# Where the tensors of a decoder kernel lie in SBUF: weights at multiples of 1 KB, activations 512 bytes past one

## The reference

```python
def first_block(x, ...):
    h = rmsnorm(x, g_pre)
    (gq, gk, gv, ga, gz, dq, dk, dv, iq, ik, iw, dz, xq, xz, gates) = split_cols(h @ w_in)   # 11352 columns
    y_gla = gla_mixer(...)      # gated linear attention, chunks of 64
    y_dsa = dsa_mixer(...)      # 128 best keys of each query, then attention
    y_mem = cross_mixer(...)    # attention to 256 memory rows
    merged = (s_gla * (y_gla @ w_gla_out) + s_dsa * (y_dsa @ w_dsa_out)
              + s_mem * (y_mem @ w_x_out))
    return x + rmsnorm(merged @ w_o, g_post)

def second_block(x, ...):       # two layers
    for l in range(2):
        main, mq = mlstm_mixer(...) if l == 0 else swa_mixer(...)
        mix = concat(main, memory_attention(mq, mk, mv)) @ w_out[l]
        x = x + rmsnorm(mix, g_mix_post[l])
        h = rmsnorm(x, g_ffn_pre[l])
        gate, up = split(h @ w_ffn_in[l])                # 1024 -> 2 x 2816
        x = x + rmsnorm((silu(gate) * up) @ w_ffn_out[l], g_ffn_post[l])   # 2816 -> 1024
        if l == 0: k_sh, v_sh = shared_kv(x, ...)
```

## The kernel before, in words

| tensor | start | start modulo 1024 |
|---|---|---|
| raw, whi, wlo | 16512, 32896, 49280 | 128, 128, 128 |
| K (identity, masks) | 65664 | 128 |
| V, gpost, small | 71424, 71872, 75968 | 768, 192, 192 |
| H, XR, R | 78016, 110784, 127168 | 192, 192, 192 |

## Time and profile before

### The profile page before, as it was taken

How to read it: one execution, slowest core, us unless ns; L and a number is a source line. 1 busy time by engine, 2 the same in 40 slices (tenths; PEclk the granted TensorE clock), 3 DMA queues, 4 the chain that set the end, 5 groups by cost and what they waited for, 6 DMA issues and landing times.

```text
span 2001.5 us, 32809 instructions
## 1 busy us (share of the span) xinstructions
PE 1968.7 (98%) x13488; PEld 1781.3 (89%) x13488; DVE 1145.0 (57%) x1595; ACT 932.6 (47%) x1647; POOL 145.5 (7%) x149
## 2 busy tenths in 40 slices
PE   8999999999999999999999999999999999999998
PEld 6798888877889778888999899999988799999998
DVE  3375347465343233353353999972377659999523
ACT  4443142355433342355454755652258856565422
POOL 0000000000000000000000233300000003333000
PEclk9999999999999999999999999999999999999999
DMA  6521122211334123332212233332231113223331
GB/s 179 146 85 64 43 84 84 85 64 59 111 112 162 63 106 105 106 116 89 81 48 80 77 125 106 106 126 95 97 116 43 64 64 116 106 106 106 127 106 64
DMA packets 29824, 191.24 MB, mean 96 GB/s; under 512 B 3689, under 2 KB 4841, under 8 KB 8562
## 3 DMA queue, kind: packets, MB, share of 16 engines
q1 hardware_dynamic: 26562, 178.58, 25.4%
q0 software_dynamic: 3120, 10.62, 2.0%
HBM read 185.38 MB, written 3.67 MB: 94 GB/s over the span
## 4 chain that ended last, share of the span: by engine, by line
PE 90%; DVE 5%; ACT 3%; issue 1%; DMA 1%; SPq 0%; DVEq 0%; ACTq 0%
PE PS L561 21%; PE PS L563 20%; PE PS L562 20%; PE PS L1034 6%; PE PS L1036 6%; PE PS L1035 6%; DVE wlo L2721 1%; ACT whi L1546 1%; PE PS L895 1%; PE PS L714 1%; PE PS L731 1%; PE PS L1152 1%; PE PS L917 1%; PE PS L851 1%; PE PS L1344 1%
## 5 line engine op out<-in xcount | busy, mean ns | idle before, releaser
L2323 DVE TENSOR_TENSOR wlo<-raw,whi 128x2048 fp32r<-128x2048 f32 (+2 forms) x117 | 264.9, 2264 | 375.3 <-ACT whi L1546 374.9
L1546 ACT ACTIVATE whi<-raw 128x2048 fp32r<-128x2048 f32 (+2 forms) x250 | 311.7, 1256 | 211.1 <-PE PS L563 190.7
L561 PE MATMUL PS<-hhi,whi 128*128 128x512 f32 (+1 forms) x768 | 313.2, 408 | 3.1 <-DVE hlo L2370 3.0
L563 PE MATMUL PS<-hhi,wlo 128*128 128x512 f32 (+1 forms) x768 | 302.7, 394 | 0.0
L562 PE MATMUL PS<-hlo,whi 128*128 128x512 f32 (+1 forms) x768 | 301.3, 392 | 0.0
L561 PE MATMUL PS<-whi,ahi 128*128 128x256 f32 x704 | 196.1, 279 | 0.0
L562 PE MATMUL PS<-wlo,ahi 128*128 128x256 f32 x704 | 196.1, 279 | 0.0
L563 PE MATMUL PS<-whi,alo 128*128 128x256 f32 x704 | 196.1, 278 | 0.0
L561 PEld LDWEIGHTS PS<-hhi,whi 128*128 128x128 f32 (+1 forms) x768 | 144.4, 188 | 40.7 <-DVE hlo L2370 5.4
L1034 PE MATMUL PS<-shi,whi 128*128 128x256 f32 x640 | 179.5, 280 | 0.9 <-DVE gated_ L2766 0.4
L1036 PE MATMUL PS<-shi,wlo 128*128 128x256 f32 x640 | 178.5, 279 | 0.0
(11 more groups left out here) (458 smaller groups left out, 4605.8 us busy)
## 6 DMA issues: line engine op xcount, KB each, us to landing
raw<-in_stream SPq DMA_DIRECT2D x165, 1024.0 KB, 4.8
gpost<-in_gposts POOLq DMA_DIRECT2D x5, 512.0 KB, 7.6
X<-in_x SPq DMA_DIRECT2D x4, 512.0 KB, 6.1
X<-in_x POOLq DMA_DIRECT2D x1, 2048.0 KB, 10.4
out<-X SPq DMA_DIRECT2D x4, 512.0 KB, 2.6
bias_line<-linet POOLq DMA_DIRECT2D x1, 1536.0 KB, 35.1
tbias<-bias_line POOLq DMA_DIRECT2D x1, 1024.0 KB, 7.5
memx<-in_mem POOLq DMA_DIRECT2D x1, 1024.0 KB, 5.4
```

Of the source, the lines that this page charges most:

```text
L561: nc.tensor.matmul(out, lh, rh, start=(k == 0), stop=False)
L563: return nc.tensor.matmul(out, ll, rh, start=False, stop=(k == n_k - 1))
L1546: return nc.scalar.activation(out_, in_, func, scale=scale)
L2323: V_.tensor_tensor(wlo[:, s % 2, :, cols_], raw[:, s % 2, :, cols_], whi[:, s % 2, :, cols_], ALU.subtract)\
```

## The change

The same tensors are allocated in another order, with two fillers that nothing uses. `K` comes first, then 256 bytes, then `raw`, `whi` and `wlo`, then 512 bytes, then the regions H, XR and R; `V`, `gpost` and `small` come behind R. No instruction is added, removed or moved on any engine, and no shape changes.

```diff
@@ -52,6 +52,10 @@
 MASK_COLS = (256, 384, 512)
+
+
+TO_KB = 64
+APART = 128
@@ -275,13 +279,12 @@
+        K = sb("K", [P, K_ALL])
+        sb("to_kb", [P, TO_KB])
         raw = sb("raw", [P, 2, KT, C])
         whi = sb("whi", [P, 2, KT, C], F32R)
         wlo = sb("wlo", [P, 2, KT, C], F32R)
-        K = sb("K", [P, K_ALL])
-        V = sb("V", [P, V_COLS])
-        gpost = sb("gpost", [P, D])
-        small = sb("small", [P, 512])
+        sb("apart", [P, APART])
@@ -417,6 +420,10 @@
         close()
+
+        V = sb("V", [P, V_COLS])
+        gpost = sb("gpost", [P, D])
+        small = sb("small", [P, 512])
```

## The result

The changed kernel takes 2025.26 us (median of 4 runs, 2024.45 to 2025.56), the kernel before 2001.82 (4 runs, 1996.54 to 2002.78). The ratio is 1.0125, with a 95% interval of 1.011 to 1.014: slower by 23 us. The forecast was 1977.2.

The account below looks back on a forecast made before the run. TensorE's matmuls, 1968.7 of 2001.5 us, were taken as the bound: 2001.5 - 27.6 (quicker pace everywhere) + 3 (waits) = 1976.9, so 1977.2 against the runs' median. Range 1930 to 2024; the forecast case's own 1970 to 1993.

Parts of the forecast that it names:

- The bound and the kind of effect: TensorE's matmul-to-matmul distances make the time; a relation of both operand streams' addresses could change them, inferred.
- Bit 9 is inert: In operand addresses: stationary operands moving by 512 bytes leave the pace unchanged, 797 matmuls at 113.2 ns; no effect.
- (1): Operand addresses of TensorE's matmuls: the quicker pace everywhere, 26.2 us from 256 columns and 1.4 from 512, 27.6 us less.
- third, longer pace: Sign of the slower case in layers' last products, besides 765 matmuls in 90 us everywhere; no size given.
- "slower" rival: Matmuls sharing a start at 0 modulo 512 keep only the slower rhythm: 24 us more, 2025; chance 0.26, by more 0.02.
- The upper end: Bound on operand addresses: all matmuls stay at or fall to the slower pace, 12.1 + 12.1, 24 us more.
- Nothing happens: Matmul rhythm set by time alone, addresses below 512 inert: 2001.8 us, within 1996 to 2008; chance 0.25.
- (2): Seven-product part at the faster rhythm: VectorE 94% busy, TensorE waits for operands; 3 us given back.
- the end without cover: Seven-product part: all 34 x 0.37 = 13 us of the gain there lost to waits.
- the other 112 are followed by a wait: Reading of 256-column matmul distances: besides 2,716 quicker and 5,907 slower ones, 112 are followed by a wait.
- (3): VectorE, ScalarE, GpSimd: VectorE's price does not know the place; value 0, or 2 us either way.
- (4): Weight stream: 165 transfers of 1 MB land 4.8 us after issue; even 1 us more each is hidden; value 0.

Follow-up runs that it names:

- w0_a64: Changed kernel with weights at 0 and activations at 64 modulo 1024 (d 64, the distance of the kernel before): 2004.9 us, ratio 1.0013 to the kernel before.
- w0_a0: Changed kernel without the 512-byte filler, weights and activations both at 0 modulo 1024 (d 0): 2026.81 us, ratio 1.0128 to the kernel before.
- the bare chains: Separate kernel of float32r matmul chains only, over d (moving operand's bytes past the stationary one, modulo 256): 256 columns 120.0 ns at d = 0, 117.8 at 64.
- w0_a256: Changed kernel with weights at 0 and activations at 256 modulo 1024: 2026.14 us, ratio 1.0124 to the kernel before.
- w0_a96: Changed kernel with weights at 0 and activations at 96 modulo 1024: 2033.39 us, ratio 1.0168 to the kernel before.
- a112: Changed kernel with weights as slices 16 bytes into their tensors, all activations 112 past them modulo 256: 2035.18 us, ratio 1.0163 to the kernel before.
- w128_a640: Changed kernel with K behind R, so weights at 128 (W, their start modulo 256) and activations at 640 modulo 1024: 2024.71 us, ratio 1.0117.
- odd_mixed: Every operand 16 past a multiple of 32, activations 64 past the weights, but the seven-product sums' operands 192 past: 1985.31 us, ratio 0.991 to the kernel before.
- rows_112: Changed kernel with weights at 0, regions H, XR and the sums at 112, rest of R at 64 modulo 256: 2006.75 us, ratio 1.0033.
- odd_192: Changed kernel with every operand 16 past a multiple of 32, distance 192 (64 in region XR): 1999.6 us, ratio 1.0003 to the kernel before.
- odd_64: Changed kernel with every operand 16 past a multiple of 32, distance 64 (192 in region XR): 1988.32 us, ratio 0.9953 to the kernel before.
- all three layouts built on the one-dimensional map: Changed kernel, weights 16 bytes into their tensors, activations 112 past, 144 past, or each moving operand 112 past where possible: 2035.18, 2013.02, 2009.63 us.
- the map: Separate kernel: chains of 30 matmuls of 256 columns over 16 stationary by 16 moving places; d = 64 takes 117.8 ns at 32 and 113.3 at 48.

## Why the prediction was wrong, and where it was right

**The bound and the kind of effect: right.** The time is the sum of TensorE's distances, and it changed by what they changed. That a relation of the two operands' places acts on them, which was inferred, is shown: w0_a64 against w0_a0 differ in 64 bytes of an unused filler and by 22 us, and the bare chains show it without other engines.

**Bit 9 is inert: right.** w0_a0, w0_a256 and the changed kernel, 0, 256 and 512 bytes apart, run at 120.0 and 226.7 to 227.4 alike. "What can act is the place within 512 bytes" was right, and wide: it is the distance within 256 bytes and the stationary operand's place within 32.

**The step that failed: the value taken in (1), "the quicker of the two paces everywhere", chosen as "nearer to the rows than either end, since each piece of it has been run by this chip".** The chip had run each of those pieces at d = 64. The change made it 0, and no row of before has anything at 0. The two paces are a pair that belongs to a distance (at d = 192 and a multiple of 32 the chains have the same pair), not the two that matmuls have; with the distance the pair went too. What stood in its place is one pace of 120.0, the "third, longer pace" that the prediction names as a sign of its "slower" rival: +28.6 us against -26.2, and for 512 columns -6.1 against -1.4.

**The upper end: its sum right by chance.** It let 2,716 matmuls fall to the slower pace (12.1 us) and 2,818 of 512 columns to 233.7 (12.1 us). The first term was mis-sized: a pace outside the pair cost all 8,623 of 256 columns, 119.94 - 116.39 = 3.55 ns each, 30.6 us by that count and 28.6 with the distances that hold waits. The second had the wrong sign. 24 and 22 lie close to each other for no reason of the argument. The real bound from above was never worked out; w0_a96 with 2033 us and a112 with 2035 show that it lay there at least. The "slower" rival's mechanism, a start common to both streams that leaves one rhythm, is as far as I can see what happened (that they start on the same foot no trace shows), but the rhythm is not "the slower", and "0 modulo 512" is 0 modulo 256 of the distance: w128_a640 has it with W = 128.

**"Nothing happens", and the conclusion drawn from the rule behind it: refuted.** The Trainium skill, "SBUF — State Buffer", section "Who interferes with whom", says that "PE and ACT never wait on anyone". The prediction read it as: placement is worth 0. Here placement is worth 22 us of 2001 in one direction (the spans) and 15 in the other (odd_mixed), with the same instructions. None of it needs another engine: the bare chains have the paces with the others idle, so what is refuted is the conclusion, not the sentence about engines. Whether the two ports themselves contend no run here shows; that the distance of what they read sets the pace, they all do.

**(2), what a faster rhythm meets: the mechanism right, its size too small.** The changed kernel never reached it. rows_112 and odd_192 did: activations moving at 113.4 to 113.9, and the distances over 130 ns in the seven-product parts cost 9.5 and 9.1 us beyond the pace, where before has 3.2. So new waits take 6 us; I had given back 3, with 13 as the end without cover. The two seven-product parts took 396.8 us before, from their first to their last start, and take 391.4 and 390.4 there: 3 us less a layer, not the 6 that I had named. It is part of why odd_192 is worth nothing; about as much comes of its weights, which move at 117.2 (610.4 us against 603.7). odd_64 has the quick pace in the long products, where VectorE is 28% busy (25 of 90 us), and nearly half of its gain from 512 columns: 0.5%.

**Two readings of the rows were wrong; neither moves the sum.** The clock was not at its upper level throughout. In four stretches of 3.4 to 10.2 us of the profiled execution before, the granted clock is 0.5, which is 1.2 GHz, and the slices of 50 us in the earlier trace rows round them away. Ahead of two of them, at 1461.7 and 1584.6 us, TensorE had been only some half busy (2.17 of 3.7 us, 2.32 of 4.6). The changed kernel has such stretches too, and the same mean clock, 0.995. One pair, before and after:
```profile
1461.70:1465.00 3.30, 3.30 (x16) 3.20 (x16) 3.30 (x6) 3.30 (x7) 0.00 (x0) 0.50 0.85 334
```
```profile
1474.60:1478.00 3.40, 3.40 (x16) 3.40 (x17) 3.40 (x6) 3.40 (x7) 0.00 (x0) 0.50 0.81 320
```
And "the other 112 are followed by a wait" is not so: 15 of these distances hold idle time of TensorE, 15 lie in such stretches of the clock, and 82, of 138 to 268 ns, show no idle time. Nor does a pace turn by a wait alone. Layer 1's seven-product part is slow from 1686.3 us, after one distance of 138 ns with no idle time in it, and TensorE waits only at 1687.6. What turns a pace is not shown.

**(3) and (4): right.** 1225 and 2290 ns of VectorE and 4.8 us of the transfers stayed, and so did 216 and 429 ns of the plain float32 matmuls.

**What stays open.** Why this distance gives this pace: the chains don't show the inside of a read, and the dependence on the number of stationary columns has no order that I can read. Why a chain settles in one of two paces at 64 and 192, and why the kernels settle more often in the slower one at 64 (117.5 in odd_64, where 10 of 16 chains have 113.3). What turns a chain or a product from one pace to the other. What most distances would do with 512 columns where the stationary operand lies 16 past a multiple of 32: only 64, 112, 144 and 192 were run there, in kernels. And operands of types other than float32r, which no map has.

## What to carry to other kernels

Where TensorE is the bound and its operands are float32r, treat the start of both operands modulo 256 bytes as a tuning parameter: measure the pace with bare chains over a grid of both places in steps of 16 bytes, and check the winner in the kernel, since all three layouts built on the one-dimensional map were slower than the kernel before. A tensor added ahead of others, or an aligned layout, moves these places without a word; compare distances of matmul starts before and after, not only times. And a pace seen at one layout is no bound for another: if the layout changes, its price has to be measured or bounded from outside the rows.

## What the runs showed of the hardware that I had not expected

A float32r matmul of 256 columns with 128 stationary ones takes 113.3 to 120.2 ns from start to start by placement alone (single chains of the map up to 123.7), one of 512 columns 226.7 to 236.7, at the upper clock. The best place for one size is not that for the other: with the stationary operand at 0, d = 0 is the quickest for 512 columns and, with 96, the slowest for 256. Sharing a start modulo 256 removes the second rhythm, and the time spreads less: four layouts with d = 0 lie between 2022.46 and 2027.6 us in 10 runs, the kernel before between 1990.64 and 2011.44 in the 82 runs beside the later experiments. Part of either spread is the clock, whose mean over a run is 0.993 to 0.999. Among runs with 0.995 it is 3.2 us (7 runs at d = 0) against 13.2 (20 runs of the kernel before). And a shorter stationary load does not always help: at d = 64 and 512 columns, 32 stationary columns take 231.1 to 231.6 ns and 128 take 228.9.
